# Two-layer MoE decoder on Trainium2: the resident expert pair moved from the 17th to the 25th, two up matrices per layer loaded by 16 narrow transfers

## The chip, the cores and the metric

One NeuronCore of one Trainium2 chip. The metric is the device time of one execution in microseconds (us), median of several runs. Before the change it is 1185.53 us (3 runs, 1184.88 to 1185.78).

## What is computed

The reference is a decoder trunk of two layers over 256 tokens of width 1024, all in float32. A layer mixes tokens by attention (a sliding window in layer 0, differential in layer 1, both with cross-attention heads into 256 memory tokens), projects the heads, normalizes, and then runs a mixture of experts: a router picks 8 of 64 experts for each token, and one shared expert sees all tokens. In the reference's words, for each expert and for the shared one:

```
h = jax.nn.silu(xb @ w_gate[e]) * (xb @ w_up[e])
return h @ w_down[e]
...
x = layer_norm(DN_ALPHA * x + f, ln_g[i, 1], ln_b[i, 1])
```

`w_gate[e]` and `w_up[e]` are 1024 x 256, `w_down[e]` is 256 x 1024: 1 MB (1024 KB) each, 192 matrices a layer. All of them are read from HBM in every execution.

## The kernel before, in words

**Units.** The kernel pads each expert to 64 slots (two tiles of 32) and works on the 64 experts of a layer in 32 pairs; one pair is one unit of the loop, numbered from 0 here. Four pairs are an octet. Pairs are the body of `unit` on TensorE (line 1409): the gate product (line 1301, 32 matrix products of 128x256 as the trace counts them), the up product (line 1328), the scatter of the pair two back into the sum banks (line 1372), the turning of the one-hot matrices and of the hidden rows (lines 1269, 1337), and the down product of the pair before (line 1364). The last pair of an octet also gathers the tokens of the next octet (line 1259, recorded under the helper's line 848 with the tile `hot`). ScalarE and VectorE apply silu, form the hidden rows, and scale the outputs. Octet 6 (pairs 24 to 27) carries the shared expert's products besides (lines 1187 and 1196). TensorE runs octet 0 written out, octets 1 to 3 as a loop, octet 4 written out, octet 5 as a loop, 6 and 7 written out (lines 1446 to 1461).

**Buffers and the order of the loads.** `store` holds 12 matrices: gate, up and down of two pairs, even pairs in one half (`b` = 0) and odd ones in the other (`pair_place`, `matrix_at`, line 312). All expert weights are issued by SyncE (SP) in one order written by hand (lines 639 to 682), each transfer behind a wait on a semaphore that tells that its buffer is free: gate matrices of pair n+2 when the gate product of pair n is done (`reload_gate`, 485), up matrices likewise (`reload_up`, 493), down matrices of pair n+1 when the down product of pair n-1 is done (`reload_down`, 466). `pair` (459) moves both experts' matrices in one transfer of 2048 KB, 128 partitions of 16 KB; `expert` (453) moves one matrix, 1024 KB. Around the start of a layer some buffers are shared with the attention's weights, so the first pairs' matrices come in pieces: among them the up matrix of the second expert of pair 2 (line 651, `expert(l, 1, 1, 1)`), which is loaded when the first pair's hidden product is done; behind it in SP's order stand the halves of pair 3's gate and up matrices (652, 653) and what follows.

**The kept pair.** One pair of each layer, number `RES_PAIR` = 16, is not loaded into `store` in the loop. Its six matrices are put before the loop starts into tiles that are idle then: `home` (gate), `lnrow` and `xT` (up), `x` and `memT` (down), by `keep` (553; calls in 613, 638, 640, 645, 648). Where its turn comes, the order has `kept=True` and only moves semaphores (665, 668). `x` is restored by GpSimd from `xhalf` when the kept pair's down product is done (815 to 819), and the norm's rows are loaded into `lnrow` once its up product is done (`load_norm`, 569).

**The end of a layer.** The last pair's up and down matrices come in halves (`last_up`, `last_down`), and TensorE's last unit is written out (1420 to 1427, `down_last`). The next layer's input weights are issued on SP behind them.

Of the kernel before, what the change touches and what calls it, by code (L numbers as in the profile page):

```python
# [16 lines left out]
P = 128  # L17
# [30 lines left out]
UNROLL = RING // 2  # L48
MATRIX = KT * HID
REGION = 6  # L50
STEPS = PAIRS // UNROLL
OCTET = 8
OCT_PAIRS = OCTET // 2
OCTETS = NE // OCTET
RES_PAIR = 16
RES_STEP = RES_PAIR // UNROLL
RES_OCTET = RES_PAIR // OCT_PAIRS
SHARED_OCTET = OCTETS - 2
FIRST_PIECES = 4
HEADS_EARLY, HEADS_LATE = slice(0, 10), slice(10, 12)  # L60
# [18 lines left out]
def build_trunk(nc, x_in, xT_in, memT_in, w_in_a, sinks, w_in_b, lambda_qk, subln_g, w_mem_kv, w_out, ln_g, ln_b,  # L79
# [60 lines left out]
    with ExitStack() as ctx:  # L140
# [277 lines left out]
        def _(sp):  # L418
# [34 lines left out]
            def expert(l, i, k, part):  # L453
# [3 lines left out]
                sp.dma_start(matrices(matrix_at(b, e, part)), src).then_inc(sem(f"{landed_name[part]}{k}_{l}"), 16)  # L457

            def pair(l, i, b, part):

                if part > 0:
                    sp.sem_inc(sem(f"{landed_name[part]}{2 * b + 1}_{l}"), 16)
                src = pair_rows(l, part, i, b).rearrange("a p e n -> (a p) (e n)")
                sp.dma_start(matrices(matrix_at(b, 0, part), 2), src).then_inc(sem(f"{landed_name[part]}{2 * b}_{l}"), 16)
# [88 lines left out]
            def keep(l, part, e):  # L553

                w = (w_gate, w_up, w_down)[part][l, RES_PAIR, :, e, :]
                sp.dma_start(resident_view(part, e), by_f(w) if part == 2 else by_k(w)).then_inc(sem(f"kept_{part}{e}"), 16)

# [22 lines left out]
            for l in range(DEPTH):  # L580
# [69 lines left out]
                sp.wait_ge(sem(f"hidden_{l}"), 1)  # L650
                expert(l, 1, 1, 1)
                reload_gate_halves(l, 2, 1, 1)
# [15 lines left out]
                reload_down(l, UNROLL * (RES_STEP - 1) + 1, RES_STEP, 0, kept=True)  # L668
                reload(l, UNROLL * (RES_STEP - 1) + 1, RES_STEP + 1, 0)
                reload_down(l, UNROLL * RES_STEP, RES_STEP, 1)  # L670
# [152 lines left out]
        def _(pe):  # L823
# [34 lines left out]
            for l in range(DEPTH):  # L858
# [423 lines left out]
                def gate(U, O, j, rs, kept, place):  # L1282
                    b, first = j % 2, place == 0
                    pe.wait_ge(s_(f"gate_landed{2 * b}"), rs * 16 + 16)
                    if place == 1:
                        pe.wait_ge(sem("gate_apart"), (l + 1) * 16)
                    if place in (2, 3):
                        pe.wait_ge(sem(f"gate_first{b}"), (l + 1) * 16)
                    for e in range(2):
                        if kept:  # L1290
                            pe.wait_ge(sem(f"kept_0{e}"), (l + 1) * 16)
                    w = [gate_view(b, e) for e in range(2)]
                    if kept:
                        w = [resident_view(0, e) for e in range(2)]
                    for k in range(KT):
                        if j == 0 and k == 0 and first:
                            chunk_out(O, 3)
                        if j == 0:
                            chunk_out(O, k)
                        for e in range(2):  # L1300
                            last = pe.matmul(gate_bank[slots_of(e), 0:HID], xg[:, k, slots_of(2 * j + e)], w[e][:, k, :],  # L1301
                                             start=(k == 0), stop=(k == KT - 1))
                        if place < 2 and k == KT // 2 - 1:
                            last.then_inc(s_("half_gated"), 1)
                    last.then_inc(s_("gated"), 1)

                def up(U, j, rs, kept, r, place, by_halves=False):
                    b = j % 2
                    pe.wait_ge(s_("hT_ready"), U + 1)
                    pe.wait_ge(s_(f"up_landed{2 * b}"), rs * 16 + 16)  # L1310
                    if not by_halves:
                        pe.wait_ge(s_(f"up_landed{2 * b + 1}"), rs * 16 + 16)
                    for e in range(2):
                        if kept:
                            pe.wait_ge(sem(f"kept_1{e}"), (l + 1) * 16)
                    w = [up_view(b, e) for e in range(2)]
# [23 lines left out]
                def down(U, b, rs, gathers, turned, kept, is_apart):  # L1340

                    w = []
                    for e in range(2):
# [4 lines left out]
                        elif kept:  # L1348
                            pe.wait_ge(sem(f"kept_2{e}"), (l + 1) * 16)
                            w.append(resident_view(2, e))  # L1350
# [58 lines left out]
                def unit(r, o, j, place=OCT_PAIRS, last=False, kept=False, kept_before=False, shared=None):  # L1409
# [10 lines left out]
                    if last:  # L1420
# [6 lines left out]
                        return  # L1427
                    up(U, j, rs, kept, r, place)
                    if place > 1:
# [16 lines left out]
                with pe.Fori(0, rounds) as r:  # L1446
                    gather(r * OCTETS, None, first_gather_bank)
                    for j in range(OCT_PAIRS):
                        unit(r, 0, j, place=j)
                    with pe.Fori(1, RES_OCTET) as o:  # L1450
                        for j in range(OCT_PAIRS):
                            unit(r, o, j)
                    for j in range(OCT_PAIRS):
                        unit(r, RES_OCTET, j, kept=(j == 0), kept_before=(j == 1))
                    with pe.Fori(RES_OCTET + 1, SHARED_OCTET) as o:
                        for j in range(OCT_PAIRS):
                            unit(r, o, j)
                    for j in range(OCT_PAIRS):
                        unit(r, SHARED_OCTET, j, shared=j)
                    for j in range(OCT_PAIRS):  # L1460
# [672 lines left out]
```

## Time and profile before

| | |
|---|---|
| median of 3 runs | 1185.53 us (1184.88 to 1185.78) |
| span of the profiled execution | 1183.3 us |
| TensorE busy (matrix products) | 1149.2 us, 97% |
| VectorE, ScalarE, GpSimd busy | 347.2, 300.0, 56.4 us |
| granted TensorE clock | 0.996 of full speed |
| moved by DMA | 449.12 MB, 380 GB/s over the span |
| chain that ended last | TensorE 85%, DMA 9%, VectorE 3% |

The span goes from the first to the last instruction of one execution; the profile gives no other time for that execution, and the median of the unprofiled runs lies 2.2 us above it. Busy time of TensorE is modelled where products are pipelined, so a stretch that shows 97% can still contain waits; the chain of waits tells where they are. In the chain a row is a piece of time and what it was spent on: an engine at a line with the number of instructions, a transfer (from its issue to its landing), or "issue", time in which the engine waited for nothing that the profile shows. Layer 0's expert loop runs from about 134 to 572 us, layer 1's from about 733 to 1171 us.

### The profile page before, as it was taken

The page shows a single profiled execution, that of the slowest core. Times are in us where ns is not written, and L with a number is a line of the kernel's source. Part 1 is how long each engine was busy: PE and PEld are TensorE (multiplying, and loading weights), DVE is VectorE, ACT ScalarE, POOL GpSimd, SP SyncE. Part 2 cuts the span into 40 slices and gives each one's busy share as a digit, 9 for nine tenths or more (in the row PEclk, how much of TensorE's full clock was granted, in tenths as well). Part 3 has the DMA queues.
Part 4 walks back from the last instruction along what each step waited for, and adds up shares of the span by engine and source line. Part 5 has one row for each costly group of instructions (what it writes and reads, how often), then busy time and mean ns, then how long its engine had stood idle before and what let it go on. Part 6 is the DMA issues. An engine that isn't in the chain of part 4 may idle for free.

```text
span 1183.3 us, 22174 instructions
## 1 busy us (share of the span) xinstructions
PE 1149.2 (97%) x8846; PEld 688.0 (58%) x8846; DVE 347.2 (29%) x912; ACT 300.0 (25%) x713; POOL 56.4 (5%) x100
## 2 busy tenths in 40 slices
PE   9999999999999999999999999999999899999995
PEld 6865755555555555554787647555555555555552
DVE  0445522222122212121523557221222222121224
ACT  1454222212122212121214533122221212221222
POOL 1431100000001000000011001000000010000000
PEclk9999999999999999999999999999999999999998
DMA  9945999999999999999990558999999999999995
GB/s 375 418 161 185 349 418 426 428 428 428 429 428 421 429 426 427 426 426 418 406 364 2 230 233 343 408 426 426 429 429 428 428 423 427 426 426 428 428 423 204
DMA packets 42732, 449.12 MB, mean 380 GB/s; under 512 B 4512, under 2 KB 4896, under 8 KB 14240
## 3 DMA queue, kind: packets, MB, share of 16 engines
q1 hardware_dynamic: 41648, 443.30, 89.8%
q10 hardware_dynamic: 1008, 4.73, 1.0%
q8 instruction: 57, 0.93, 0.3%
q14 instruction: 19, 0.16, 0.0%
HBM read 446.96 MB, written 1.05 MB: 379 GB/s over the span
## 4 chain that ended last, share of the span: by engine, by line
PE 85%; DMA 9%; DVE 3%; ACT 1%; issue 1%; DVEq 0%; SPq 0%; ACTq 0%
PE bank L1301 18%; PE bank L1328 17%; PE bank L1364 17%; PE bank L848 7%; PE bank L867 6%; PE bank L1372 5%; PE bank L906 4%; DMA store<-in_w_gate 4%; DMA store<-in_w_down 3%; DMA store<-in_w_in_b 2%; PE bank L1337 2%; PE bank L1196 1%; PE bank L1066 1%; PE bank L1077 1%; ACT work L1498 1%
## 5 line engine op out<-in xcount | busy, mean ns | idle before, releaser
L1301 PE MATMUL bank<-store,work 128*64 128x256 f32 x1984 | 227.8, 382 | 5.3 <-DMA store<-in_w_gate 5.3
L1328 PE MATMUL bank<-store,work 128*64 128x256 f32 x1952 | 225.3, 379 | 6.2 <-issue 6.2
L1364 PE MATMUL bank<-store,work 128*32 128x512 f32 x1888 | 218.4, 595 | 3.1 <-ACT work L1498 2.9
L1301 PEld LDWEIGHTS bank<-store,work 128*64 128x64 f32 x1984 | 137.0, 137 | 116.1 <-issue 41.1
L1328 PEld LDWEIGHTS bank<-store,work 128*64 128x64 f32 x1952 | 145.0, 137 | 75.7 <-issue 11.6
L2030 DVE SCALAR_TENSOR_TENSOR yhalf<-bank,gcol,yhalf 128x512 fp32r<-128x512 f32 x124 | 92.9, 751 | 219.1 <-ACT yhalf L1664 219.1
L2022 DVE TENSOR_TENSOR work<-work,bank 128x256 f32<-128x256 f32 x64 | 27.0, 422 | 346.9 <-PE bank L1328 346.9
L1664 ACT ACTIVATE yhalf<-bank,gcol 128x512 fp32r<-128x512 f32 x124 | 85.1, 688 | 172.1 <-PE bank L1364 172.1
L1364 PEld LDWEIGHTS bank<-store,work 128*32 128x32 f32 x1888 | 56.1, 109 | 122.4 <-issue 110.7
L1498 ACT ACTIVATE work<-bank 128x512 f32<-128x512 f32 (+4 forms) x177 | 78.0, 441 | 105.8 <-PE bank L848 47.3
L1498 ACT ACTIVATE back<-bank 128x128 fp32r<-128x128 bf16 x64 | 17.8, 278 | 282.0 <-PE bank L1269 282.0
L867 PE MATMUL bank<-xT,store 128*128 128x256 f32 x352 | 77.9, 380 | 0.7 <-DMA store<-in_w_in_b 0.7
L1372 PE MATMUL bank<-yhalf,back 64*128 64x512 f32 x504 | 75.7, 418 | 0.0
L1742 DVE COPY work<-bank 128x512 f32<-128x512 f32 (+3 forms) x77 | 51.5, 672 | 70.8 <-PE bank L848 41.2
L867 PEld LDWEIGHTS bank<-xT,store 128*128 128x128 f32 x352 | 66.2, 190 | 10.4 <-DMA store<-in_w_in_b 1.1
L1654 ACT ACTIVATE work<-bank 128x256 f32<-128x256 f32 x64 | 24.6, 385 | 184.3 <-PE bank L1301 184.3
L848 PE MATMUL bank<-hot,xhalf 128*128 128x256 f32 x512 | 69.4, 290 | 1.0 <-DVE xhalf L1895 0.9
L848 PEld LDWEIGHTS bank<-hot,xhalf 128*128 128x128 f32 x512 | 64.0, 189 | 4.6 <-issue 2.1
L1372 PEld LDWEIGHTS bank<-yhalf,back 64*128 64x128 f32 x504 | 42.4, 184 | 30.1 <-issue 23.8
L906 PE MATMUL bank<-store,work 128*128 128x512 f32 x128 | 57.8, 594 | 0.0
L906 PEld LDWEIGHTS bank<-store,work 128*128 128x128 f32 x128 | 23.2, 190 | 23.4 <-issue 23.1
L819 POOL TENSOR_TENSOR x<-xhalf 128x1024 f32<-128x1024 f32 x4 | 9.6, 2426 | 475.3 <-PE bank L1364 475.3
(185 smaller groups left out, 822.7 us busy)
## 6 DMA issues: line engine op xcount, KB each, us to landing
store<-in_w_down SPq DMA_DIRECT2D x56, 2048.0 KB, 17.7
store<-in_w_gate SPq DMA_DIRECT2D x56, 2048.0 KB, 17.7
store<-in_w_up SPq DMA_DIRECT2D x52, 2048.0 KB, 19.2
store<-in_w_up SPq DMA_DIRECT2D x18, 1024.0 KB, 10.5
store<-in_w_gate SPq DMA_DIRECT2D x12, 1024.0 KB, 8.5
store<-in_w_in_b SPq DMA_DIRECT2D x3, 3072.0 KB, 22.4
store<-in_w_out SPq DMA_DIRECT2D x4, 2048.0 KB, 14.2
store<-in_w_down SPq DMA_DIRECT2D x6, 1024.0 KB, 11.7
```

The costliest lines, as they stand in the source:

```text
L848: last = pe.matmul(dst, a, b, start=(n == 0), stop=(n == len(pairs) - 1))
L867: mm = pe.matmul(bank_at(g)[:, c * 256:(c + 1) * 256], w[:, k, c0 + c * P:c0 + (c + 1) * P], moving[:, k, :], start=(k == 0), stop=(k == K ...
L906: last = pe.matmul(bank_at(g)[:], mixT[:, c, t * P:(t + 1) * P], item_view((l, f"out{half}"), 512)[:, c, :], start=start, stop=(done == KT))
L1301: last = pe.matmul(gate_bank[slots_of(e), 0:HID], xg[:, k, slots_of(2 * j + e)], w[e][:, k, :], start=(k == 0), stop=(k == KT - 1))
L1328: last = pe.matmul(up_bank[slots_of(e), 0:HID], xg[:, k, slots_of(2 * j + e)], w[e][:, k, :], start=(k == 0), stop=(k == KT - 1))
L1364: last = pe.matmul(yb[half][rows_of(t, e), :], hT[b][:, f, slots_of(e, t)], w[e][:, f, half * 512:half * 512 + 512], start=(f == 0), stop= ...
L1372: pe.matmul(sums[2 * t + half][:], back[b][rows_of(t), :], yhalf[rows_of(t), n, half * 512:half * 512 + 512], start=False, stop=False)
L1498: return act.activation(dst, src, ACT.Copy)
L1664: act.activation(yhalf[:, 0, half * 512:half * 512 + 512], yb[half][:], ACT.Copy, scale=gcol[:, j:j + 1])\
L1742: return dve.tensor_copy(dst, src)
L2022: dve.tensor_tensor(hidrow, sg, up_bank[:, 0:HID], ALU.mult).then_inc(s_("h_ready"), 1)
L2030: dve.scalar_tensor_tensor(out=yhalf[:, 1, part], in0=yb[half][:], scalar=gcol[:, j:j + 1], in1=yhalf[:, 0, part].bitcast(F32), op0=ALU.mu ...
```

## The change

The kept pair becomes number 24, the first of octet 6, which is also the octet with the shared expert. TensorE's octets 1 to 5 become one loop. On SP the kept pair's place in the order moves with `RES_STEP` (from 8 to 12). The up matrix of the second expert of pair 2 and of pair 26 is loaded by `narrow_up`: 16 transfers of 8 partitions (64 KB) each, counted by one semaphore `narrow`, for which TensorE waits before the up product; pair 26's other up matrix is loaded by itself. The two semaphores of each kept kind of matrix become one.

```diff
--- before.py
+++ after.py
@@ -47,15 +47,17 @@
 PAIRS = NE // 2
 UNROLL = RING // 2
 MATRIX = KT * HID
+NARROW = 8
+NARROW_PARTS = P // NARROW
 REGION = 6
 STEPS = PAIRS // UNROLL
 OCTET = 8
 OCT_PAIRS = OCTET // 2
 OCTETS = NE // OCTET
-RES_PAIR = 16
+RES_PAIR = 24
 RES_STEP = RES_PAIR // UNROLL
-RES_OCTET = RES_PAIR // OCT_PAIRS
 SHARED_OCTET = OCTETS - 2
+assert RES_PAIR == SHARED_OCTET * OCT_PAIRS
 FIRST_PIECES = 4
 HEADS_EARLY, HEADS_LATE = slice(0, 10), slice(10, 12)
 MASKED = -1.0e32
@@ -456,6 +458,13 @@
                 src = pair_rows(l, part, i, b)[:, :, e, :].rearrange("a p n -> (a p) n")
                 sp.dma_start(matrices(matrix_at(b, e, part)), src).then_inc(sem(f"{landed_name[part]}{k}_{l}"), 16)
 
+            def narrow_up(l, i):
+
+                sp.sem_inc(sem(f"up_landed1_{l}"), 16)
+                src = w_up[l, UNROLL * i, :, 1, :]
+                for p in range(0, P, NARROW):
+                    sp.dma_start(matrices(matrix_at(0, 1, 1))[p:p + NARROW], src[p:p + NARROW]).then_inc(sem("narrow"), 16)
+
             def pair(l, i, b, part):
 
                 if part > 0:
@@ -553,7 +562,7 @@
             def keep(l, part, e):
 
                 w = (w_gate, w_up, w_down)[part][l, RES_PAIR, :, e, :]
-                sp.dma_start(resident_view(part, e), by_f(w) if part == 2 else by_k(w)).then_inc(sem(f"kept_{part}{e}"), 16)
+                sp.dma_start(resident_view(part, e), by_f(w) if part == 2 else by_k(w)).then_inc(sem(f"kept_{part}"), 16)
 
             rows = [[(biasrow[:], router_bias.rearrange("(o a) b -> o a b", o=1).broadcast_to([P, DEPTH, NE])),
                      (wr, by_row_run(w_router[0]))],
@@ -648,7 +657,7 @@
                 keep(l, 2, 0)
                 reload_gate_halves(l, 1, 1, 0)
                 sp.wait_ge(sem(f"hidden_{l}"), 1)
-                expert(l, 1, 1, 1)
+                narrow_up(l, 1)
                 reload_gate_halves(l, 2, 1, 1)
                 reload_up_halves(l, 2, 1, 1)
                 reload_down(l, 1, 1, 0)
@@ -666,7 +675,9 @@
                 reload_down(l, UNROLL * (RES_STEP - 1), RES_STEP - 1, 1)
                 reload(l, UNROLL * (RES_STEP - 1) + 2, RES_STEP, 1)
                 reload_down(l, UNROLL * (RES_STEP - 1) + 1, RES_STEP, 0, kept=True)
-                reload(l, UNROLL * (RES_STEP - 1) + 1, RES_STEP + 1, 0)
+                reload_gate(l, UNROLL * (RES_STEP - 1) + 1, RES_STEP + 1, 0)
+                expert(l, RES_STEP + 1, 0, 1)
+                narrow_up(l, RES_STEP + 1)
                 reload_down(l, UNROLL * RES_STEP, RES_STEP, 1)
                 reload(l, UNROLL * RES_STEP + 2, RES_STEP + 1, 1)
                 reload_down(l, UNROLL * RES_STEP + 1, RES_STEP + 1, 0)
@@ -1288,7 +1299,7 @@
                         pe.wait_ge(sem(f"gate_first{b}"), (l + 1) * 16)
                     for e in range(2):
                         if kept:
-                            pe.wait_ge(sem(f"kept_0{e}"), (l + 1) * 16)
+                            pe.wait_ge(sem("kept_0"), (l + 1) * 2 * 16)
                     w = [gate_view(b, e) for e in range(2)]
                     if kept:
                         w = [resident_view(0, e) for e in range(2)]
@@ -1304,15 +1315,17 @@
                             last.then_inc(s_("half_gated"), 1)
                     last.then_inc(s_("gated"), 1)
 
-                def up(U, j, rs, kept, r, place, by_halves=False):
+                def up(U, j, rs, kept, r, place, by_halves=False, narrow=0):
                     b = j % 2
+                    if narrow:
+                        pe.wait_ge(sem("narrow"), (2 * l + narrow) * NARROW_PARTS * 16)
                     pe.wait_ge(s_("hT_ready"), U + 1)
                     pe.wait_ge(s_(f"up_landed{2 * b}"), rs * 16 + 16)
                     if not by_halves:
                         pe.wait_ge(s_(f"up_landed{2 * b + 1}"), rs * 16 + 16)
                     for e in range(2):
                         if kept:
-                            pe.wait_ge(sem(f"kept_1{e}"), (l + 1) * 16)
+                            pe.wait_ge(sem("kept_1"), (l + 1) * 2 * 16)
                     w = [up_view(b, e) for e in range(2)]
                     if kept:
                         w = [resident_view(1, e) for e in range(2)]
@@ -1346,7 +1359,7 @@
                             pe.wait_ge(sem("down_apart"), (l + 1) * 16)
                             w.append(apart)
                         elif kept:
-                            pe.wait_ge(sem(f"kept_2{e}"), (l + 1) * 16)
+                            pe.wait_ge(sem("kept_2"), (l + 1) * 2 * 16)
                             w.append(resident_view(2, e))
                         else:
                             w.append(down_view(b, e))
@@ -1425,7 +1438,7 @@
                         turn_h(U)
                         down_last(r, U, b)
                         return
-                    up(U, j, rs, kept, r, place)
+                    up(U, j, rs, kept, r, place, narrow=1 if place == 2 else 2 if shared == 2 else 0)
                     if place > 1:
                         scatter(U - 2, (j - 2) % OCT_PAIRS)
                     turn_back(U + 1, OCTET * o + 2 * j + 2, 1 - b)
@@ -1447,16 +1460,11 @@
                     gather(r * OCTETS, None, first_gather_bank)
                     for j in range(OCT_PAIRS):
                         unit(r, 0, j, place=j)
-                    with pe.Fori(1, RES_OCTET) as o:
+                    with pe.Fori(1, SHARED_OCTET) as o:
                         for j in range(OCT_PAIRS):
                             unit(r, o, j)
                     for j in range(OCT_PAIRS):
-                        unit(r, RES_OCTET, j, kept=(j == 0), kept_before=(j == 1))
-                    with pe.Fori(RES_OCTET + 1, SHARED_OCTET) as o:
-                        for j in range(OCT_PAIRS):
-                            unit(r, o, j)
-                    for j in range(OCT_PAIRS):
-                        unit(r, SHARED_OCTET, j, shared=j)
+                        unit(r, SHARED_OCTET, j, kept=(j == 0), kept_before=(j == 1), shared=j)
                     for j in range(OCT_PAIRS):
                         unit(r, OCTETS - 1, j, last=(j == OCT_PAIRS - 1))
                     pe.wait_ge(s_("y_parted"), r * (2 * PAIRS) + (2 * PAIRS - 1))
```

## Rows read from the trace of the kernel before

**Rows 1.** The page, costliest groups: busy us, mean ns of one | idle before

```profile
PE 1149.2 (97%) x8846; PEld 688.0 (58%) x8846; DVE 347.2 (29%) x912; ACT 300.0 (25%) x713; POOL 56.4 (5%) x100
...
L848 PE MATMUL bank<-hot,xhalf 128*128 128x256 f32 x512 | 69.4, 290 | 1.0 <-DVE xhalf L1895 0.9
...
L819 POOL TENSOR_TENSOR x<-xhalf 128x1024 f32<-128x1024 f32 x4 | 9.6, 2426 | 475.3 <-PE bank L1364 475.3
```

**Rows 2.** Chain of waits, 289 to 362 us: start us, us, what

```profile
301.71 3.63 PE bank L1301 x32
...
305.62 24.42 DMA store<-in_w_gate
...
330.08 3.67 PE bank L1301 x32
...
348.20 3.60 PE bank L1301 x32
```

**Rows 3.** Chain of waits, 445 to 575 us

```profile
454.74 3.60 PE bank L1301 x32
...
467.21 3.60 PE bank L1301 x32
...
481.41 3.60 PE bank L1301 x32
...
497.07 3.60 PE bank L1301 x32
...
515.22 3.60 PE bank L1301 x32
...
527.47 3.60 PE bank L1301 x32
```

**Rows 4.** DMA view, 220 to 340 us: packets; instruction queue (packets, MB, share)

```profile
DMA packets 3529, 51.41 MB, mean 428 GB/s; under 512 B 391, under 2 KB 391, under 8 KB 391
...
q8 instruction: 1, 0.02, 0.1%
```

**Rows 5.** Layer 1, timeline of TensorE: gate products of pairs 15, 24 and 31

```profile
928.27 1.95 PE L1301 MATMUL bank<-store,work 128*64 128x256 f32 x16 [0.88 <-DMA store<-in_w_gate]
...
1052.84 3.46 PE L1301 MATMUL bank<-store,work 128*64 128x256 f32 x30
...
1151.22 2.16 PE L1301 MATMUL bank<-store,work 128*64 128x256 f32 x17 [0.88 <-DMA store<-in_w_gate]
```

**Rows 6.** Pair 31, layer 0: gate product; its transfer's issue, and us to landing

```profile
553.69 3.67 PE L1301 MATMUL bank<-store,work 128*64 128x256 f32 x32 [0.88 <-DMA store<-in_w_gate]
...
531.12 0.33 SPq L464 DMA_DIRECT2D store<-in_w_gate  x1
...
store<-in_w_gate SPq DMA_DIRECT2D x1, 2048.0 KB, 22.5
```

**Rows 7.** Pair 24, layer 0: issue of its gate matrices, and us to landing

```profile
429.76 0.33 SPq L464 DMA_DIRECT2D store<-in_w_gate  x1
...
store<-in_w_gate SPq DMA_DIRECT2D x1, 2048.0 KB, 19.6
```

**Rows 8.** DMA view, 340 to 450 us: instruction queue

```profile
q8 instruction: 7, 0.11, 0.4%
```

**Rows 9.** Timeline of TensorE, start of layer 1

```profile
596.69 3.50 PE L867 MATMUL bank<-xT,store 128*128 128x256 f32 x15 [0.70 <-DMA store<-in_w_in_b]
```

**Rows 10.** Pairs 2 and 3, layer 0: SP's issues, landing of the first, chain

```profile
141.80 0.34 SPq L457 DMA_DIRECT2D store<-in_w_up  x1
...
150.03 0.54 SPq L532 DMA_DIRECT2D store<-in_w_up  x1
...
store<-in_w_up SPq DMA_DIRECT2D x1, 1024.0 KB, 8.4
...
157.72 3.45 PE bank L1328 x32
...
166.34 3.60 PE bank L1301 x32
```

## The prediction

> **What bounds the kernel now.** I read the page first, then the chain of waits through the expert loop of layer 0, then landing times of single transfers. The page [rows 1] shows TensorE busy 97% in its matrix products, at a clock of 0.996. DMA is as full [rows 4], so the question at each place is which of the two is late. The chain of waits gives TensorE's own pace: its L1301 rows are the starts of the gate products of pairs 13, 15 and 16 [rows 2] and 24 to 29 [rows 3]. A pair with nothing to wait for takes 12.25 us (28 to 29); the last of an octet has the gather too (L848 on hot, 69.4 us for 16 gathers [rows 1], 4.3 each) and takes 16.6. That is 53.3 us an octet, 13.3 a pair. Pairs 24 to 27 also carry the shared expert and take 12.5, 14.2, 15.7 and 18.2.
>
> A pair's weights are 3 transfers of 2048 KB (2.097 MB). The DMA view of the stretch 220 to 340 us moves 428 GB/s [rows 4], so one takes 4.90 us and a pair 14.7: DMA loses 1.4 us a pair to TensorE. What pays for this is a lead: buffers filled before the loop, and the kept pair, which costs the loop no transfer. In the trace the first lead is gone by pair 14. The gate matrices of pair 15, issued at 305.6, land 24.4 us later at 330.0, and the gate product begins at 330.08 [rows 2]; layer 1 does the same at 928.27 [rows 5]. From 301.7 to 348.2 this costs 46.5 us where TensorE's pace is 12.25 + 12.25 + 16.6 = 41.1: 5.4 us of waiting. Then pair 16 comes out of SBUF and TensorE is ahead by a pair again. That lead lasts to pair 30: pair 31's gate product begins at 553.7, when its transfer (531.1 plus 22.5) lands [rows 6], 1.8 us late. So a layer waits 7.2 us in all, and reaches its end with the lead just spent.
>
> **The kept pair at 24.** The stream keeps its order, but pair 16 is now in it and pair 24 not. Every pair from 17 to 23 therefore lands one pair (14.7 us) later than now. Pair 23's gate matrices take the place of pair 24's, issued at 429.8 and landed 19.6 us later, at 449.4 [rows 7]. Buffers don't hold this back: in the stretch where TensorE waits, issue is 24.4 us ahead of landing. So pair 23 can't begin before 449.4. It is the last of its octet, and waits for its up matrices as pair 15 does: gate of 15 to gate of 16 is 348.2 - 330.1 = 18.1 us [rows 2]. Pair 24 then begins at 467.5 instead of 454.7 [rows 3].
>
> One correction goes the other way. From 340 to 450 us the instruction queue loads 7 packets of 16 KB, against 1 in the 120 us before, where TensorE ran its loop over octets 1 to 3 [rows 4, 8]. With octets 1 to 5 in one loop I expect almost none. From pair 15's gate (330.0) to pair 24's (449.4) are 24 transfers: 24 x 4.90 = 117.6 us, so 447.6 without them. Pair 24 then begins at 465.7, 11.0 us late. In layer 1 the same sum from 928.2 gives 1045.8, plus 18.1 is 1063.9, against 1052.84 [rows 5]: 11.1 late.
>
> From pair 24 on, TensorE has a lead of a pair, and its own work is 12.5 + 14.2 + 15.7 + 18.2 + 3 x 12.25 = 97.3 us to the gate of pair 31, the first five as the chain has them [rows 3]. That is 465.7 + 97.3 = 563.0. Its transfer landed at 553.6 already and still will: TensorE is now the bound, with 9 us of lead that nothing uses. The 1.8 us wait at pair 31 goes; 563.0 - 553.7 = 9.3 us remain. I find no such wait in the tail behind it, and one in the next layer's projection, 0.7 us at 596.69 [rows 9], which goes: **8.6 us**. All that is issued by the buffers' release moves with TensorE. Layer 1: 1063.9 + 97.3 = 1161.2, against 1151.2 [rows 5]: **10.0 us**, as nothing follows that could absorb it. Together 18.6 us. The kept pair thus pays for the lead when little of the loop is left: it saves a wait of 1.8 us and adds 11 earlier.
>
> The other parts of the move: GpSimd's restoring of x (L819, 2 x 2.4 us a layer [rows 1]; it waits on GpSimd, whose queue holds nothing more in that layer) now waits for pair 24, some 60 us before the layer's end; the norm rows wait for pair 24 too, and the layer's end is later still. Zero, covered by seven pairs; without cover at most 4.9 us a layer. Summed semaphores of the kept loads: the loads landed long before. The semaphore of the narrow pairs is one wait more ahead of TensorE's up products of pairs 2 and 26; behind it on TensorE stand the up product, the scatter and the down product, and VectorE waits for the first. Zero, once it has landed.
>
> **The narrow transfers.** The up matrix of pair 2's second expert is now one transfer of 1024 KB. It takes half of 4.90, 2.45 us, of the stream, is issued at 141.8 and has landed at 150.2; TensorE needs it at 157.7 [rows 10]. Sixteen issues cost SP 0.34 to 0.54 us each (the short and the long issue of rows 10), 5.4 to 8.6 us, and end at 147.2 to 150.4. Behind them on SP stand the halves of pair 3's gate and up matrices, the last of which goes out at 150.03 now and by 152.6 then; pair 3 needs them from 166.3 on. SP's delay is thus covered twice. In the second case, pair 26, SP issues at some 466 with two transfers still queued ahead, and behind it stands pair 25's down matrix, whose buffer is free only at 474 or later: zero.
>
> What the transfers themselves cost no row shows: all transfers of the trace go to 128 partitions. Bounds: in rows 4, 391 small packets are 16 per transfer; the others carry 51.41 MB in 3138 packets, 16 KB each, one per partition's run. A transfer of eight runs has eight packets, so at most eight of sixteen engines work on it. If the eight change from transfer to transfer, the cost is 0. If the engines that get it are otherwise ahead, and the slow ones are relieved, it is down to -2.45. If they are always the same eight, each carries 16 packets instead of 8, and what is behind lands 2.45 us later. If its packets block one another so that only one or two engines' worth moves, 1.05 MB takes 19.6 us at 2/16 of 428 GB/s, 17.1 more than now; at 1/16, 39.2 us. I take +2.45: nearest to rows where an engine moves at its own pace. This falls wholly on the path: the stream is the bound at pair 23, and every landing is later. Twice 2.45 is 4.9 us. Pair 26's narrow matrix falls where TensorE is the bound by 9 to 11 us: zero, unless it costs more than that.
>
> The Trainium skill (DMA: Bandwidth & Descriptors, "Why a DMA increments its semaphore by 16 and not by 1") says that a copy from SP with 8 as its slowest dimension runs on the eight lowest-numbered engines, always the same ones; by that rule too the sum has 2.45. No run here shows it.
>
> **Sum.** The profiled execution's span is 1183.3; the median of the runs is 1185.5, 2.2 above it, which I carry over. 1183.3 + 18.6 + 4.9 = 1206.8, plus 2.2 is **1209.0 us**.
>
> **Rivals.**
> - *The narrow transfers block one another*, chance 0.2. Eight adjacent partitions are loaded at a time; if where a packet lands limits it, four engines share one way in and a narrow matrix takes 19.6 us. TensorE waits some 9 us at pair 2, the stream is 17.1 late at pair 23, and 34.3 late behind pair 26, which eats the 9 us of lead: pair 31's gate lands at 553.6 - 1.8 + 34.3 = 586.1, 32.4 later than now; some 33 in layer 1, where fewer code packets are saved (1.0 us). 1185.5 + 65.5 = 1251. For it: 428 GB/s is a ceiling, and no row says whose. Against: engines that are a little apart in time reach different partitions and free one another; then the cost is between, 5 to 12 us a time, 1214 to 1230. The Trainium skill (SBUF — State Buffer, "Door 1: The DMA port swizzle") has partitions 0 to 7 on two of 16 ports at 27.2 GB/s each; by it the full price would be paid. No row here tests it.
> - *The layer's end is set by bytes, not by TensorE*, 0.05. DMA is full to the end now; were it late behind pair 24 as well, moving the pair would lose nothing, and the code packets saved (449.4 - 447.6 = 1.8 us, at most, in either layer) would leave 1182. It decides where TensorE's work from pair 24 to 31 is less than the DMA's; the rows say 97.3 us against 6 x 14.7 = 88 for the pairs from 25 to 31's gate, which is why I hold it unlikely.
> - *The narrow part changes nothing* (engines rotate, or those relieved were late), 0.15: 1204.1, or 1199.2 with -2.45 a layer. Inside the range.
>
> **How the numbers follow.** Forecast 0.6, rivals 0.2, 0.05, 0.15. The range reaches from 1199 to 1240: the bounds below, and the between values of the first rival above; left out are its full price (0.12) and the second rival (0.05), with 0.03 for what I haven't thought of. 0.2% (2.4 us) is about what a measurement can tell from no change. Faster 0.04 and within 0.02 are the second rival, alone or half cancelled by the narrow transfers; slower 0.94.
>
> **What would show it.** Gate products of pair 14 to 23 each beginning as their transfer lands, pair 24's at some 468 instead of 454.7; no wait for DMA at pairs 25 to 31; DMA below 428 GB/s in the last pairs of a layer; fewer instruction packets. Wrong if the wait of pair 15 doesn't go on, if pair 31 still waits for its gate matrices, or if pair 2's up product waits for the narrow matrix (then it blocks).

## The result, and the profile after

The changed kernel takes 1213.23 us (median of 5 runs, 1211.5 to 1215.8), against 1185.51 us in the same comparison: a ratio of 1.0234, 95% interval 1.022 to 1.0247, 27.7 us slower. The forecast was 1209.0, 23.5 us slower, with a range of 1199 to 1240. The profiled execution took 1211.5 us, and its span is 1209.7 us, 26.4 above the span before. So the direction and most of the size were right; some 4 us were not in the sum, and the runs below show which term was short.

The page of the changed kernel. Its gate product is now line 1312 and its up product line 1341:

```profile
PE 1151.8 (95%) x8846; PEld 692.5 (57%) x8846; DVE 347.1 (29%) x912; ACT 299.6 (25%) x713; POOL 56.0 (5%) x100
...
DMA packets 43453, 448.87 MB, mean 371 GB/s; under 512 B 4992, under 2 KB 5376, under 8 KB 14720
...
q8 instruction: 42, 0.69, 0.2%
...
PE 77%; DMA 16%; DVE 3%; issue 2%; ACT 1%; DVEq 0%; SPq 0%; ACTq 0%
...
L1312 PE MATMUL bank<-store,work 128*64 128x256 f32 x1984 | 227.8, 382 | 13.4 <-DMA store<-in_w_gate 13.4
```

TensorE's busy time is nearly what it was (1149.2 before). What changed is the chain: DMA has 16% of it instead of 9, TensorE 77 instead of 85. The work is the same, and more of it waits for a transfer.

The chain of waits of the changed kernel, first where the waiting begins in layer 0 (238 to 300 us), the counterpart of [rows 2]; columns are start us, us, what:

```profile
247.89 3.63 PE bank L1312 x32
...
251.69 24.54 DMA store<-in_w_gate
...
276.27 3.67 PE bank L1312 x32
...
294.40 3.60 PE bank L1312 x32
```

The product that begins at 276.27, behind the transfer, is that of pair 11, not of pair 15: the same pattern, a gate product that begins as its transfer lands, four pairs earlier. It goes on in every octet up to pair 23. Pair 2's up product, which the prediction named as a place where a wait would mean blocking, does not wait: from gate to gate pair 2 takes 12.2 us as before. The same view from 445 to 600 us, the counterpart of [rows 3]:

```profile
427.90 24.53 DMA store<-in_w_gate
...
452.47 3.67 PE bank L1312 x32
...
470.59 3.60 PE bank L1312 x32
...
483.06 3.60 PE bank L1312 x32
...
497.26 3.60 PE bank L1312 x32
...
512.93 3.60 PE bank L1312 x32
...
531.08 3.60 PE bank L1312 x32
...
543.31 3.60 PE bank L1312 x32
...
555.54 3.60 PE bank L1312 x32
...
567.78 3.60 PE bank L1312 x32
```

Pair 23 begins at 452.5 as its matrices land, pair 24 at 470.6 instead of 454.7, and from there to pair 31 there is no wait for a transfer: 567.78 - 470.59 = 97.2 us, where the prediction's sum had 97.3. DMA moves 407 GB/s from 540 to 572 us, in the last pairs of layer 0, less than the 428 as said; but the kernel before had only 422 from 526 to 558 too, so this sign tells little.

Where each layer stands is best seen counted from the gate product of its own pair 0. In us, from the timelines of TensorE, for this kernel and those of the experiments:

| kernel | median | layer 0, pair 24 | pair 31 | layer 1, pair 24 | pair 31 |
|---|---|---|---|---|---|
| before | 1185.5 | 320.4 | 419.4 | 320.2 | 418.6 |
| changed | 1213.2 | 336.7 | 433.9 | 335.2 | 432.4 |
| k24_wide | 1204.6 | 331.9 | 429.1 | 332.3 | 429.5 |
| k24_wide_b | 1203.7 | 331.6 | 428.9 | 331.8 | 429.0 |
| k24_first | 1211.0 | 336.5 | 433.7 | 335.1 | 432.4 |
| k24_second | 1203.4 | 331.7 | 428.9 | 332.0 | 429.2 |
| k24_spread | 1216.7 | 338.1 | 435.3 | 338.4 | 435.6 |
| k24_by16 | 1209.0 | 334.9 | 432.1 | 333.9 | 431.1 |
| k24_wide_out | 1206.3 | 332.9 | 430.1 | 332.1 | 429.3 |
| k16_second | 1201.0 | 320.3 | 425.3 | 320.6 | 428.2 |
| k20 | 1193.4 | 327.7 | 424.9 | 326.4 | 423.6 |
| k12 | 1185.6 | 318.1 | 419.0 | 318.8 | 419.5 |

### The profile page after: what moved, and what is told of

Its sections match the earlier page's. It is cut to its first block, busy times and chain, and to the rows that moved or that the text cites. A ratio compares the mean times of both kernels' runs of the same rounds, so it can differ in the third digit from the quotient of the medians.

```text
span 1209.7 us, 22242 instructions
## 1 busy us (share of the span) xinstructions
PE 1151.8 (95%) x8846; PEld 692.5 (57%) x8846; DVE 347.1 (29%) x912; ACT 299.6 (25%) x713; POOL 56.0 (5%) x100
## 2 busy tenths in 40 slices
DMA packets 43453, 448.87 MB, mean 371 GB/s; under 512 B 4992, under 2 KB 5376, under 8 KB 14720
## 4 chain that ended last, share of the span: by engine, by line
PE 77%; DMA 16%; DVE 3%; issue 2%; ACT 1%; DVEq 0%; SPq 0%; ACTq 0%
PE bank L1312 17%; DMA store<-in_w_gate 16%; PE bank L1341 14%; PE bank L1377 14%; PE bank L878 7%; PE bank L859 7%; PE bank L1385 4%; PE bank L917 4%; PE bank L1350 1%; PE bank L893 1%; PE bank L1207 1%; PE bank L1077 1%; PE bank L1088 1%; ACT work L1506 1%; PE bank L1190 1%
## 5 line engine op out<-in xcount | busy, mean ns | idle before, releaser
L1312 PEld LDWEIGHTS bank<-store,work 128*64 128x64 f32 x1984 | 137.0, 137 | 124.8 <-issue 33.5
L1341 PEld LDWEIGHTS bank<-store,work 128*64 128x64 f32 x1952 | 149.9, 137 | 90.5 <-issue 34.3
```

The costliest lines, as they stand in the source:

```text
L1341: last = pe.matmul(up_bank[slots_of(e), 0:HID], xg[:, k, slots_of(2 * j + e)], w[e][:, k, :], start=(k == 0), stop=(k == KT - 1))
```

## The experiments

### The kept pair alone, and one narrow load at a time

`k24_wide` is the changed kernel with the narrow loads undone:

```diff
-                narrow_up(l, 1)
+                expert(l, 1, 1, 1)
...
-                narrow_up(l, RES_STEP + 1)
+                expert(l, RES_STEP + 1, 1, 1)
...
-                    up(U, j, rs, kept, r, place, narrow=1 if place == 2 else 2 if shared == 2 else 0)
+                    up(U, j, rs, kept, r, place, narrow=0)
```

> The changed kernel with both narrow loads put back as one transfer of 128 partitions; only the kept pair's move stays. Theory (the kept pair at 24 costs 18.6 us, the narrow loads the rest): 1204 us, pair 24's gate product of layer 0 at about 466 us instead of 454.7, no wait for DMA from pair 24 on. Rival (the narrow loads are the whole loss, since they delay the stream in every layer, and the kept pair's place is free because bytes set the end): 1182 to 1186 us.

Measured: 1204.59 us, ratio 1.015 (1.0133 to 1.0167) to the kernel before, 19.0 us slower in its comparison; the same kernel once more (`k24_wide_b`) gave 1203.67, 18.5 slower. The prediction's term for the kept pair was 18.6. In the trace of `k24_wide_b` pair 24's gate product begins at 465.6, in that of `k24_wide` at 466.7, where pair 0 is 0.9 us later too; 465.7 was forecast. The chain of waits of `k24_wide_b` from 455 to 575 us has no transfer in it:

```profile
465.56 3.60 PE bank L1312 x32
...
478.04 3.60 PE bank L1312 x32
...
492.24 3.60 PE bank L1312 x32
...
507.92 3.60 PE bank L1312 x32
...
526.07 3.60 PE bank L1312 x32
```

`k24_first` keeps only pair 2's narrow load, `k24_second` only pair 26's; in each the other `narrow_up` is `expert` again, and TensorE's wait counts `(l + 1) * NARROW_PARTS * 16`.

> The changed kernel with only pair 2's narrow load; pair 26's is one transfer again. Theory (the second narrow load falls where TensorE is the bound and is free): no different from the changed kernel, 1213 us within 1. Rival (both cost alike, half of 9 us each): about 1208.5 us.

> The changed kernel with only pair 26's narrow load; pair 2's is one transfer again. Theory: as with both loads wide, 1204 us within 1, although the transfer behind the narrow one (pair 25's down matrix) still lands some 13 us after the one ahead of it. Rival (both cost alike): about 1208.5 us.

Measured: 1210.96 and 1203.35 us, in the same comparison as `k24_wide` with 1204.59. Pair 2's load carries the loss, 6.4 to 7.6 us by these medians, and pair 26's costs nothing that can be told; the rival, both alike, falls. `k24_first` was expected at 1213 within 1 and came out 2 us lower. Its trace reads like that of the changed kernel (pair 31 at 433.7 and 432.4), whose own five executions spread over 4.3 us, so nothing in the expert loops shows a difference. By the table the changed kernel's pair 31 is 5.1 us later than in `k24_wide_b` in layer 0 (433.9 - 428.9, rounded from 433.93 - 428.86) and 3.4 in layer 1.

`k16_second` puts a narrow load for pair 26 into the kernel before, where the kept pair is 16:

```diff
+                with sp.Fori(RES_STEP + 1, STEPS - 4) as i:
+                    step(i)
+                step(STEPS - 4, narrow=True)
+                step(STEPS - 3)
...
+                        expert(l, i + 1, 0, 1)
+                        narrow_up(l, i + 1)
```

> The kernel before (kept pair 16) with pair 26's second up matrix loaded by 16 transfers of 8 partitions, pair 2's left whole. Theory (a narrow load costs the stream some 6 us beyond a wide one, and is free only where TensorE is behind the stream; with the kept pair at 16 the stream is the bound at pair 31): 6 us a layer, 1197.5 us, and pair 31's gate product waits some 8 us for its matrices. Rival (near the end of a layer a narrow load is hidden whatever the kept pair's place, as it was with 24): 1185.6 us.

Measured: 1200.97 us, ratio 1.0122 (1.0107 to 1.0138). The rival falls: the very load that is free with the kept pair at 24 costs 15.4 us with it at 16, where 12 was expected. The place of the wait was not as expected either. In layer 0 pair 31 doesn't wait; the up product of pair 26 waits for its own narrow matrix, as the timeline of TensorE shows:

```profile
481.51 3.67 PE L1319 MATMUL bank<-store,work 128*64 128x256 f32 x32
491.21 5.23 PE L1348 MATMUL bank<-store,work 128*64 128x256 f32 x32 [6.02 <-DMA store<-in_w_up]
```

Pair 26 thus takes 23.5 us from gate to gate instead of 15.7, and pair 31's gate product begins 5.9 us later than in the kernel before (425.3 against 419.4), since the 1.8 us wait there is gone. The wait is 6.0 of these 7.8 us. Another 1.6 is the up product itself, 5.23 us instead of 3.6: behind the wait TensorE's granted clock was half (1.2 GHz), as the row of 491.21 to 494 us has it (the last three figures are clock, DMA share and GB/s):

```profile
491.21:494.00 2.79, 2.79 (x14) 1.65 (x16) 0.00 (x0) 0.00 (x0) 0.00 (x0) 0.50 0.99 423
```

In layer 1 the wait is 7.3 us, and pair 31 is 9.6 us late.

### What a narrow load costs, and why

In the changed kernel the matrix next to pair 26's narrow one, issued at 471.16, lands at 485.1, and the transfer behind it, issued at 483.19, at 498.6. From SP's timeline and the DMA view:

```profile
471.16 0.43 SPq L459 DMA_DIRECT2D store<-in_w_up  x1
471.70 5.36 SPq L466 DMA_DIRECT2D store<-in_w_up  x16
483.19 0.35 SPq L473 DMA_DIRECT2D store<-in_w_down  x1
...
store<-in_w_up SPq DMA_DIRECT2D x1, 1024.0 KB, 14.0
...
store<-in_w_down SPq DMA_DIRECT2D x1, 2048.0 KB, 15.4
```

Between the two landings lie 13.5 us; less 4.9 for the 2048 KB transfer, the narrow megabyte has taken 8.6, an estimate, where by the same rate a wide one takes 2.45 and eight engines at full pace would take 4.9. SP isn't what holds it up here: 16 issues took 5.4 us in all, 0.34 each, and were over by 477.1, before the first narrow packet. The DMA view of 487 to 491 us says where the time went; first the changed kernel, then `k24_wide_b`:

```profile
DMA packets 119, 0.83 MB, mean 207 GB/s; under 512 B 47, under 2 KB 47, under 8 KB 47
...
q1 hardware_dynamic: 119, 0.83, 103.6%
```

```profile
DMA packets 120, 1.72 MB, mean 430 GB/s; under 512 B 15, under 2 KB 15, under 8 KB 15
...
q1 hardware_dynamic: 120, 1.72, 100.6%
```

All sixteen engines are busy in both, and move half as much in the first. Not only the narrow rows are slow: by the trace's records of packets, 8 KB packets take 0.6 to 0.7 us there instead of 0.31, and the 16 KB packets of the transfer behind, which the other eight engines have by then, 1.3 instead of 0.61. (The records don't name the engine; that it is the other eight is inferred.) The first half of the narrow rows, partitions 0 to 63, had passed at 0.42 us a packet (median); the second half has 0.64.

That it is eight engines follows from the page: small packets rise from 4512 to 4992, by 480. A wide transfer leaves 16 of them; if a narrow one leaves 8, sixteen leave 128, and 4 x (128 - 16), plus 2 x 16 for pair 26's other matrix now loaded by itself, is 480. With the Trainium skill's rule (DMA: Bandwidth & Descriptors, "Why a DMA increments its semaphore by 16 and not by 1"), by which such a copy runs on eight engines, this agrees.

At pair 2, where the load costs something, there is more to it. The halves of pair 3's gate matrices stand behind the sixteen issues on SP, and go out later for it. From SP's timeline, first the changed kernel, then `k24_wide_b`:

```profile
141.36 5.41 SPq L466 DMA_DIRECT2D store<-in_w_up  x16
146.81 0.55 SPq L530 DMA_DIRECT2D store<-in_w_gate  x1
```

```profile
141.37 0.34 SPq L459 DMA_DIRECT2D store<-in_w_up  x1
144.35 0.55 SPq L530 DMA_DIRECT2D store<-in_w_gate  x1
```

From 137.5 to 146.8 us SP issues nothing but the narrow transfers, and the engines that don't carry them run out of work. From 145 to 149 us, in the same order (the last two figures of a row are DMA's share and GB/s):

```profile
145.00:149.00 4.00, 4.00 (x40) 2.64 (x38) 0.00 (x0) 0.38 (x1) 0.00 (x0) 1.00 0.60 169
```

```profile
145.00:149.00 4.00, 4.00 (x40) 2.70 (x38) 0.00 (x0) 0.39 (x1) 0.00 (x0) 1.00 0.99 387
```

A share of 0.60 instead of 0.99 for 4 us is 1.6 us of idle engines; in layer 1 the same stretch has 0.64 instead of 0.98, 1.4 us. So of the 5.1 and 3.4 us that the load costs, some 1.6 and 1.4 are, by this estimate, engines without work, and only the rest is slow packets. How much of the idling would go if SP issued faster, no run here separates from the load's being on eight engines.

`k24_spread` keeps eight partitions a transfer, but takes every fourth:

```diff
-                for p in range(0, P, NARROW):
-                    sp.dma_start(matrices(matrix_at(0, 1, 1))[p:p + NARROW], src[p:p + NARROW]).then_inc(sem("narrow"), 16)
+                for p in [h + r for h in range(0, P, 32) for r in range(4)]:
+                    sp.dma_start(matrices(matrix_at(0, 1, 1))[p:p + 29:4], src[p:p + 29:4]).then_inc(sem("narrow"), 16)
```

> The changed kernel, still 16 transfers of 8 partitions for each narrow load, but each takes every fourth partition of a group of 32 instead of eight adjacent ones. Theory (adjacent partitions share a way into SBUF, so the packets of one transfer hinder one another; in the changed kernel 8 KB packets took up to 0.7 us instead of 0.31): packets back at 0.31 us, the narrow load costs the eight engines 2.45 us more than a wide one, 1209 us. Rival (it is the eight engines and the small transfers as such): the same packets of 0.7 us, 1213 us.

Measured: 1216.71 us, 3.5 slower than the changed kernel, not 4 faster: the total was missed. SP's timeline shows what the expectation left out:

```profile
141.94 10.84 SPq L466 DMA_DIRECT2D store<-in_w_up  x16
152.83 0.61 SPq L530 DMA_DIRECT2D store<-in_w_gate  x1
```

An issue with a stride over partitions took 0.68 us instead of 0.34, so the halves of pair 3's gate matrices went out at 152.8 instead of 146.8, and the engines ran dry (36% busy from 146 to 152 us). The packets themselves, at pair 26, where all was queued, were right for one half and wrong for the other: 0.31 us up to 486.8, 0.61 after. The switch comes where the partitions pass 64. Against the changed kernel the stride thus helped the first half, 0.31 instead of 0.42, and hardly the second, 0.61 instead of 0.64. `k24_spread_rev` has the order `(64, 96, 0, 32)` instead:

> The run with every fourth partition, in the other order: partitions 64 to 127 first, 0 to 63 last. In that run the packets behind pair 26 took 0.31 us up to some 486.8 us, then 0.61 us, with the 16 KB packets of the transfer behind at 1.2. Theory (the first eight engines then share the ways in of partitions 64 to 127 with the other eight engines, which are at the next transfer): with those partitions first, done before the next transfer starts, the packets stay at 0.31 us throughout and the 16 KB packets at 0.61. Rival (any two transfers side by side slow each other): the second half is again at 0.61 us.

Measured: 1217.12 us (two executions). The slow half moved with the partitions: slow first, fast last, so the rival (any two transfers side by side) falls. The theory falls too: it had these eight engines meet the other eight on the way to partitions 64 to 127, and expected 0.31 us where they are alone there. They took 0.49 to 0.59 us from 485.2 to 486.9, when the matrix ahead was through and the first packet of the transfer behind had not started (it starts at 486.91). The DMA view from 485.2 to 486.8 us has no packet over 8 KB; below it is that of `k24_spread` from 485.2 to 486.1, its partitions 0 to 63 alone:

```profile
DMA packets 55, 0.25 MB, mean 159 GB/s; under 512 B 24, under 2 KB 24, under 8 KB 24
```

```profile
DMA packets 52, 0.21 MB, mean 237 GB/s; under 512 B 26, under 2 KB 26, under 8 KB 26
```

So these eight engines load partitions 64 to 127 slowly without any company. The DMA view of this run, 487 to 491 and 491 to 494 us:

```profile
DMA packets 134, 0.85 MB, mean 213 GB/s; under 512 B 55, under 2 KB 55, under 8 KB 55
...
q1 hardware_dynamic: 134, 0.85, 97.3%
```

```profile
DMA packets 141, 1.20 MB, mean 399 GB/s; under 512 B 49, under 2 KB 49, under 8 KB 49
...
q1 hardware_dynamic: 141, 1.20, 96.7%
```

`k24_by16` sets `NARROW = 16`, eight transfers of sixteen adjacent partitions:

> The changed kernel with 8 transfers of 16 adjacent partitions instead of 16 of 8. All sixteen engines take part, one row each. Theory (adjacent rows land through a few shared ways in): 8 KB packets above 0.31 us, a cost left at pair 2's load, 1206 to 1210 us. Rival (what counts is only that eight engines carry it all): packets of 0.31 us, no cost, 1204 us as with wide loads.

Measured: 1209.03 us, ratio 1.0198 (1.0182 to 1.0213). Against the two runs of the wide kernel 4.4 to 5.4 us of the loss stay by the medians, where the changed kernel has 8.6 to 9.6; by the table, at pair 31 against `k24_wide_b`, 3.3 and 2.1 us, where it has 5.1 and 3.4. The DMA view of 146 to 151 us, when pair 2's load runs:

```profile
DMA packets 260, 1.01 MB, mean 202 GB/s; under 512 B 99, under 2 KB 99, under 8 KB 174
...
q1 hardware_dynamic: 260, 1.01, 99.0%
```

Half the rate at full business again, and the rival falls: the loss does not need eight engines to carry it all. Nothing idles here (99% from 145 to 149 us), and the difference to the changed kernel, 1.8 and 1.3 us, is about the idle time that was counted above. The Trainium skill (SBUF — State Buffer, "Door 1: The DMA port swizzle") has four adjacent partitions on one of 16 ports, partitions 0 to 63 on eight of them and 64 to 127 on the other eight. The runs agree with that in three ways: adjacent partitions are slower, every fourth one of 0 to 63 runs at 0.31 us, and the change comes at 64. They disagree with its full price: 19.6 us by 2 of 16 ports, 8.6 measured, so that successive transfers seem to overlap in part. One rival is untested: the rows read from HBM go with the partitions in every run (eight adjacent partitions read eight adjacent rows, every fourth partition every fourth row), so that the runs can't tell the way into SBUF from the way out of HBM.

### The place of the kept pair, and the program of TensorE

`k20` and `k12` are the kernel before with `RES_PAIR` 20 and 12 (in `k20` the loop over octet 5 is dropped, as nothing is left for it).

> The kernel before with the kept pair at 20 instead of 16, nothing narrow. Theory (the stream is the bound up to the kept pair, TensorE after it): pair 24's gate product some 5.5 us late, 3.8 us of it left at pair 31, 1192 us. Rival (the place is free as long as the octet of the shared expert follows it): 1185 us.

> The kernel before with the kept pair at 12. Theory (the lead is not yet spent there, so no wait at pairs 14 to 16, but the end of a layer is set by the bytes either way): 1183 to 1185.5 us, with the waits for DMA moved to pairs 26 to 31. Rival (an early kept pair fills the buffers and the DMA engines go idle, which the end then lacks): 1187 us or more; then DMA falls below 420 GB/s behind pair 12.

Measured: `k20` 1193.38 us, ratio 1.0061 (1.0046 to 1.0076); `k12` 1185.64, ratio 1.0 (0.9991 to 1.0009). `k20` is 7.8 us slower than before, where 1192 us, some 6.5 slower, was expected; pair 31 is 5.5 and 5.0 us late where 3.8 was forecast, and pair 24 7.3 and 6.2 where 5.5 was. Of the latter 1.8 and 0.8 us are there at pair 15 already, ahead of anything that the kept pair's place should change; from there on the loss is 5.5 in both layers. In `k12` layer 0 has no wait at pairs 14 to 16, as expected (pair 15 is 4.0 us earlier than before), but the waits begin again at pairs 23 and 24, not at 26, as its chain shows (434.21 is pair 23's gate product):

```profile
411.92 22.25 DMA store<-in_w_gate
...
434.21 3.67 PE bank L1301 x32
```

Pair 24 is still 2.3 us ahead of the kernel before (318.1 against 320.4), and the up products of pairs 25 to 27 and pair 31 wait again, so that pair 31 comes at 419.0, where it came at 419.4 before; the end is set by the bytes. With the kept pair at 12, 16, 20 and 24 the kernel takes 1185.6, 1185.5, 1193.4 and 1204: flat as long as the stream is still the bound at the end, and then steep. No version beat the kernel before.

`k24_wide_out` is `k24_wide` with TensorE's octets as before the change:

```diff
-                    with pe.Fori(1, SHARED_OCTET) as o:
+                    with pe.Fori(1, 4) as o:
                         for j in range(OCT_PAIRS):
                             unit(r, o, j)
+                    for j in range(OCT_PAIRS):
+                        unit(r, 4, j)
+                    with pe.Fori(5, SHARED_OCTET) as o:
+                        for j in range(OCT_PAIRS):
+                            unit(r, o, j)
```

> The kernel with the kept pair at 24 and nothing narrow once more, as the neighbour of the next run on the same chip: 1204.6 us again, within 1.5.

> The same with TensorE's program as before the change: octets 1 to 3 a loop, 4 written out, 5 a loop. Theory (instruction packets of 16 KB each take the slowest engine's time while the stream is the bound; the prediction gave 1.8 us for them in layer 0 and 1.0 in layer 1): 2 to 3 us slower than with the loop, pair 24's gate product of layer 0 1.8 us later, 57 instruction packets instead of 42. Rival (they are lost in the other packets): no difference, under 0.5 us.

Measured: 1206.25 against 1203.67 us, 2.6 slower, with 57 instruction packets against 42. The direction holds, the size less surely: by the table it is 1.3 us in layer 0 and 0.3 in layer 1 up to pair 24, not 1.8 and 1.0, and about 0.6 lies before the first expert, which may be scatter between executions. Two traces of the same kernel, `k24_wide` and `k24_wide_b`, differ by 0.3 and 0.5 us at the same places. From pair 15 to pair 23 alone, where the stream is the bound throughout, the same timelines have 119.0 us instead of 117.5 in both layers, a difference of 1.6 and 1.5 us.

## Why the prediction was right, and where it was short

- **The stream is the bound up to the kept pair, TensorE after it.** Right. `k24_wide_b` shows it alone: pair 24 11.2 us late (331.6 against 320.4) where 11.0 was worked out, 9.5 left at pair 31 where it was 9.3; in layer 1 11.6 and 10.4, where it was 11.1 and 10.0. The place of a transfer in the order, read from the kernel before, gave the landing in the kernel after.
- **What is left over goes at the transition.** The wait of 0.7 us went as said, and the distance from pair 31 to the next layer's pair 0 fell by 1.2.
- **Fewer code packets.** Right in direction and about in size: 2.6 us by the medians of `k24_wide_out`, 3.1 where the stream is the bound, 1.6 by pair 24; 2.8 was worked out.
- **The second narrow load is free.** Right, by `k24_second`, and for the stated reason, by `k16_second`.
- **SP's issues are covered.** Right for each issue (0.34 us), and right against the time at which TensorE needs pair 3. Not right against the stream, which is what counts by the prediction's own argument that every later landing is on the path: at pair 2 the issues held the next transfer back from 144.35 to 146.81, in a stretch in which engines idled. In `k24_spread`, at 0.68 us an issue, 36% busy for 6 us is 3.8 us of idling, of 6.5 lost by pair 24 of layer 0.
- **The first narrow load costs 2.45 us a layer.** This is the term that was mis-sized. The step was "I take +2.45: nearest to rows where an engine moves at its own pace". The engines do not move at their own pace: 8 KB packets took 0.42 us and then 0.64 instead of 0.31, the transfer behind ran at half rate beside them, some engines had nothing to do meanwhile, and the stream was 5.1 and 3.4 us later. That is 8.4 us by the gate products instead of 4.9; by the medians 6.4 to 7.6 in one comparison (`k24_first`) and 8.6 to 9.6 across comparisons. The first rival had the mechanism, blocking, but at full price more than twice too high; its in-between case, 5 to 12 us a time, was where layer 0 came out, and its 1214 lies just above the 1213.2 measured. That the forecast came within 4 us in spite of the wrong mechanism here is luck: 2.45 a layer was a choice between bounds, and the measured price happened to lie near it.
- **The rival on the other side** (the end is set by bytes whatever the kept pair's place) falls by `k24_wide` and `k20`. It is true of 12 and 16, which is why the kernel before is where it is.

The rest, 27.7 less 18.5 to 19.0 for the kept pair and 8.4 for the narrow load, is under 1 us, less than the runs of the changed kernel scatter.

What stays open: why these eight engines are slow at partitions 64 to 127 even alone, and whether what slows adjacent rows lies in SBUF or in HBM. The share of adjacency itself is shown by one pair of traces at partitions 0 to 63 (0.42 against 0.31). `k24_by16`, in which all sixteen engines load both halves, doesn't separate it from which engine loads which half. And why pair 2's narrow load costs 5.1 us in layer 0 but 3.4 in layer 1.

## What to carry to other kernels

Where a stream of loads is slower than the engine it feeds, a resident block is a lead of one block: it pays only for what comes after it, so it belongs early enough that the stream is the bound again before the end; the loss from a late place can be worked out by shifting landings in the trace by one pair's transfers. Before you count a cost once per occurrence, ask at each occurrence which side is behind: the same narrow load cost nothing with the kept pair at 24 and 15.4 us, over both layers, with it at 16. Where the stream is the bound, a later issue counts against the stream, not against the engine that needs the data. And load all 128 partitions with one transfer: with few of them the engines looked busy here and moved half.

## What the runs showed that I had not expected

- While a transfer of few partitions runs to partitions 64 to 127, the transfer behind it is slow too: 207 GB/s at 103.6% busy against 430 at 100.6%. Beside one to every fourth partition of 0 to 63, as `k24_spread_rev` has it from 491 us on, the 16 KB packets are back at 0.61 us.
- Eight engines alone took 0.49 to 0.59 us for an 8 KB packet to partitions 64 to 127, and 0.31 for one to every fourth of 0 to 63.
- Issuing a transfer of eight partitions with a stride of four took SP 0.68 us instead of 0.34.
- TensorE's loop over five octets caused no instruction packet between 340 and 450 us, where 7 came when one of the octets was written out.
